# Half sums in four row groups, and rotation tables made behind the first head's key copies, in a two-layer diffusion backbone

## The chip, the core and the metric

The kernel runs on one NeuronCore of a Trainium2 chip. The metric is the device time of one execution in microseconds, as the median of several runs. TensorE (PE in the profile; its weight loads are PEld) multiplies, VectorE (DVE) and ScalarE (ACT) do the elementwise work, SyncE (SP) issues most of the DMAs, and ACT issues the others. GpSimd (POOL) only clears some buffers at the start. The program is written by hand, one instruction stream per engine, and the engines meet only at semaphores.

## The reference

```python
for i in range(DEPTH):                       # DEPTH = 2
    shift, scale, gate = adaln(c, ada_w[i], ada_b[i])
    shift_c, scale_c, gate_c = adaln(c_ctx, ada_w[i], ada_b[i])
    h = rmsnorm(x, norm_w[i]) * (1.0 + scale[:, None]) + shift[:, None]
    hc = rmsnorm(ctx, norm_w[i]) * (1.0 + scale_c) + shift_c
    if i % N_MIXERS == 0:
        y, yc = gla_mixer(h, hc, ...)        # layer 0: gated linear attention
    else:
        y, yc = diff_mixer(h, hc, ...)       # layer 1: differential softmax attention
    x = x + gate[:, None] * y
```

`adaln(cond, w, b)` is `silu(cond) @ w + b`, split into shift, scale and gate; `w` is 2048 x 6144 in each layer, and it is applied to two conditions, `c` and `c_ctx`. In layer 1 the queries and keys are normalised, multiplied by the weights `qn_w` and `kn_w`, and rotated: `t * cos + rot * sin`. There are 256 latent tokens and 256 context tokens, with 2048 features, all in float32.

## The kernel before

**Projections.** Each large product is cut into chunks of 512 output columns; a chunk has 8 pairs of 128 contraction rows. Chunks are numbered through the program: 0 to 11 are layer 0's projections (three for each of four heads), 12 to 15 its output product (`OUT0` = 12), 16 to 31 layer 1's projections (two for each of eight heads, `DIFF` = 16: keys and values, then queries and gates), and 32 to 35 its output product. In this text (16, 4) is pair 4 of chunk 16. Every weight pair goes through four steps: SP loads it into `w_raw`, ACT copies it, rounded, to `w_hi` (`split`, L558), DVE subtracts the two into `w_lo` (`low`, L1353), and PE multiplies (`project_pair`, L988). The buffers have four slots (`RING`), so that `split` of pair n+4 waits for PE to have finished pair n (`pair_done`), and PE's pair n waits for its `low` (`w_split`). A pair over four token tiles is 24 matmuls; one over two token tiles (queries and gates of layer 1) is 12. After a chunk the banks are copied out, and the next chunk's first matmul into a bank waits for `freed`.

**Modulation in the background.** Shift, scale and gate of layer 1, and the gate of layer 0, are made beside the projections. DVE multiplies tiles of `ada_w` (128 rows x 1024 columns, 512 KB) by the column of `silu(cond)` and adds them up in `ada_acc`, once for each condition m = 0, 1 (`weigh`, L1376 and L1378). One part of 2048 columns takes two halves of 1024 columns, each of 16 tiles; `HALVES` = 8 halves are numbered i = 0 to 7: gate of layer 0 (i = 0, 1), shift (2, 3), scale (4, 5) and gate (6, 7) of layer 1. SP loads tile m+2 only once DVE has weighed tile m (L411). When a half is complete, PE adds up its 128 partitions (`half_sums`, L948): four matmuls, for conditions m and column blocks b of 512, with a stationary operand of 32 columns of which one is all ones, and the results land in bank 7. In the kernel before the two conditions of a column block add into the same 32 rows of the bank, and even and odd halves use different row groups (0 and 32, or 64 and 96). Then either ACT copies the 64 rows to `ada_rows` (`half_rows`, L615, for i = 2 to 5) or DVE adds them to `gate_sums` (`add_half`, L1386, for the others). `column_sum` (L958) turns `ada_rows` into columns by a matmul with the selection matrix `sel`. `SUM_AT` says behind which pair PE does a half sum: (3, 3), (6, 1), (9, 1), (12, 1), (13, 5), (15, 3), (22, 6) and (28, 6). `SUM_OUT`, four pairs later in ACT's and DVE's order, is where the result is taken out. `COLUMNS_AT` puts the column sums behind (12, 5) and (15, 5).

**Into layer 1.** While PE does chunk 16 (keys and values of head 0), ACT and DVE make the modulated activations (`high1`, `remainder1`). Then ACT issues six small DMAs for cos, sin and the two normalising weights (L864 to L867), and waits for `rope_ok` before the first `split` of chunk 17. DVE waits for these DMAs (`rows_in`), multiplies the weights into the tables (L1743, and L1738 in `swapped`), signals `rope_ok`, and only then does `low` of (17, 0) to (17, 2) and copies out the banks of chunk 16 (`keys`, L1774). `silu_ag[:, 0]` holds the query weights until the tables are made, and is overwritten by the first Silu of head 0.

## Time and profile before

| | us |
|---|---|
| median of 3 runs | 1655.83 |
| range of the runs | 1652.74 to 1656.56 |
| the profiled execution | 1650.39 |
| its span, first to last instruction | 1648.6 |
| PE busy | 1591.9 |
| DVE busy | 1137.4 |
| ACT busy | 561.2 |

PE is busy nearly all the time, and its stretches of waiting are few and short. The columns of a timeline are start, duration, engine, line, operation, operands and count, with the idle time ahead of it in brackets; adjacent like instructions are merged. Matmul durations overlap, since they are pipelined: the time that one takes is the distance from its start to the next one's. A float32 matmul leaves two records, a matmul on float32r operands (L988) one.

### The profile page before, as it was taken

The page shows a single profiled execution, that of the slowest core. Times are in us where ns is not written, and L with a number is a line of the kernel's source. Part 1 is how long each engine was busy: PE and PEld are TensorE (multiplying, and loading weights), DVE is VectorE, ACT ScalarE, POOL GpSimd, SP SyncE. Part 2 cuts the span into 40 slices and gives each one's busy share as a digit, 9 for nine tenths or more (in the row PEclk, how much of TensorE's full clock was granted, in tenths as well). Part 3 has the DMA queues.
Part 4 walks back from the last instruction along what each step waited for, and adds up shares of the span by engine and source line. Part 5 has one row for each costly group of instructions (what it writes and reads, how often), then busy time and mean ns, then how long its engine had stood idle before and what let it go on. Part 6 is the DMA issues. An engine that isn't in the chain of part 4 may idle for free.

```text
span 1648.6 us, 18774 instructions
## 1 busy us (share of the span) xinstructions
PE 1591.9 (97%) x7392; PEld 1248.2 (76%) x7392; DVE 1137.4 (69%) x1720; ACT 561.2 (34%) x836; POOL 2.2 (0%) x9
## 2 busy tenths in 40 slices
PE   4899999999999999999999899999999999999998
PEld 2457877787778778867787677878777888788777
DVE  4338776877586659677796576777676768575864
ACT  4214332433243323532223333232323323232532
POOL 0000000000000000000000000000000000000000
PEclk9799999999999999999999899999999999999999
DMA  9993445345444354347765134445444454252554
GB/s 329 382 379 111 154 141 158 116 149 156 139 132 138 117 166 142 102 120 279 227 216 181 63 116 148 144 150 172 149 141 153 153 157 149 90 167 77 166 165 129
DMA packets 164228, 268.70 MB, mean 163 GB/s; under 512 B 11446, under 2 KB 95344, under 8 KB 162956
## 3 DMA queue, kind: packets, MB, share of 16 engines
q1 hardware_dynamic: 159072, 256.29, 48.3%
q10 hardware_dynamic: 5068, 11.22, 2.1%
q8 instruction: 58, 0.95, 0.2%
q14 instruction: 30, 0.25, 0.0%
HBM read 265.34 MB, written 2.12 MB: 162 GB/s over the span
## 4 chain that ended last, share of the span: by engine, by line
PE 86%; DVE 6%; DMA 5%; issue 1%; ACT 1%; SPq 1%; ACTq 1%; DVEq 0%
PE bank L988 68%; PE bank L1326 4%; DMA ada_w<-in_ada_w 3%; PE bank L1111 2%; PE bank L1164 2%; PE bank L1281 2%; PE bank L1265 2%; DVE ada_w L1378 1%; PE bank L924 1%; DVE w_lo L1353 1%; DMA u<-in_ctx 1%; PE bank L948 1%; DMA u<-in_ada_w 1%; PE bank L1107 1%; DVE work L1683 1%
## 5 line engine op out<-in xcount | busy, mean ns | idle before, releaser
L988 PE MATMUL bank<-w_lo,acts_hi 128*128 128x512 f32 x1536 | 613.8, 400 | 9.7 <-DVE work L1774 4.4
L988 PE MATMUL bank<-w_hi,acts_lo 128*128 128x512 f32 x1536 | 601.3, 391 | 0.0
L988 PE MATMUL bank<-w_hi,acts_hi 128*128 128x512 f32 x1536 | 601.1, 391 | 0.0
L558 ACT ACTIVATE w_hi<-w_raw 128x1024 fp32r<-128x1024 f32 x288 | 302.9, 1057 | 754.2 <-PE bank L988 673.8
L1353 DVE TENSOR_TENSOR w_lo<-w_raw,w_hi 128x1024 fp32r<-128x1024 f32 x288 | 350.3, 1221 | 277.5 <-ACT w_hi L558 277.1
L988 PEld LDWEIGHTS bank<-w_lo,acts_hi 128*128 128x128 f32 x1536 | 290.1, 189 | 85.9 <-issue 16.2
L988 PEld LDWEIGHTS bank<-w_hi,acts_lo 128*128 128x128 f32 x1536 | 290.1, 189 | 61.8
L988 PEld LDWEIGHTS bank<-w_hi,acts_hi 128*128 128x128 f32 x1536 | 290.5, 189 | 59.8 <-issue 1.9
L1378 DVE SCALAR_TENSOR_TENSOR ada_w<-ada_w,silu_p 128x1024 f32<-128x1024 f32 x210 | 261.4, 1280 | 27.2 <-DMA ada_w<-in_ada_w 23.9
L988 PE MATMUL bank<-acts_hi,w_lo 128*128 128x512 f32 x256 | 104.1, 407 | 4.3 <-DVE acts_lo L1472 4.3
L988 PE MATMUL bank<-acts_lo,w_hi 128*128 128x512 f32 x256 | 101.0, 395 | 0.0
L988 PE MATMUL bank<-acts_hi,w_hi 128*128 128x512 f32 x256 | 101.0, 395 | 0.0
L988 PEld LDWEIGHTS bank<-acts_hi,w_lo 128*128 128x128 f32 x256 | 49.0, 191 | 23.2 <-issue 13.5
L988 PEld LDWEIGHTS bank<-acts_hi,w_hi 128*128 128x128 f32 x256 | 49.1, 192 | 10.4 <-issue 0.7
L988 PEld LDWEIGHTS bank<-acts_lo,w_hi 128*128 128x128 f32 x256 | 48.8, 191 | 10.5
L1326 PE MATMUL bank<-w_lo,acts_hi 128*128 128x512 f32 x128 | 51.1, 399 | 4.3 <-DVE acts_lo L1804 3.6
L1326 PE MATMUL bank<-w_hi,acts_lo 128*128 128x512 f32 x128 | 49.9, 390 | 0.0
L1326 PE MATMUL bank<-w_hi,acts_hi 128*128 128x512 f32 x128 | 49.9, 390 | 0.0
L1164 PE MATMUL bank<-work 128*128 128x512 f32 x96 | 41.8, 592 | 0.0
L1111 PEld LDWEIGHTS bank<-work 128*64 128x64 f32 (+1 forms) x512 | 37.8, 150 | 4.9
L1111 PE MATMUL bank<-work 128*64 128x64 f32 (+2 forms) x512 | 40.7, 256 | 0.0
L1164 PEld LDWEIGHTS bank<-work 128*128 128x128 f32 x96 | 18.2, 190 | 21.4 <-issue 21.1
(185 smaller groups left out, 1247.4 us busy)
## 6 DMA issues: line engine op xcount, KB each, us to landing
ada_w<-in_ada_w SPq DMA_DIRECT2D x156, 512.0 KB, 4.4
w_raw<-in_diff_w_in SPq DMA_DIRECT2D x256, 256.0 KB, 3.0
w_raw<-in_gla_w_in SPq DMA_DIRECT2D x64, 512.0 KB, 3.8
w_raw<-in_gla_w_in SPq DMA_DIRECT2D x64, 256.0 KB, 3.1
u<-in_ada_w SPq DMA_DIRECT2D x32, 512.0 KB, 9.9
w_raw<-in_gla_w_out SPq DMA_DIRECT2D x32, 512.0 KB, 4.7
w_raw<-in_diff_w_out SPq DMA_DIRECT2D x32, 512.0 KB, 4.7
u<-in_x SPq DMA_DIRECT2D x2, 1024.0 KB, 6.5
```

Of the source, the lines that this page charges most:

```text
L558: act.activation(w_hi[:, p % RING], raw[:, p % RING], ACT.Copy).then_inc(w_hi_ok, 1)
L924: last = pe.matmul(bank[6 + q % 2][32 * j:32 * j + 32, :], silu_p[:, 2 * i + j // 2, :], quad_slot[slot][:, j, :], start=(i == 0), stop=(i ...
L948: last = pe.matmul(bank[7][row:row + 32, :], sel[:, 13 - m:45 - m], ada_acc[:, m, b * CW:(b + 1) * CW], start=(m == 0), stop=(m == 1 or i ...
L988: last = pe.matmul(bank[b][:], a, w, start=(k == 0 and i == 0), stop=(k == NK - 1 and i == 2))
L1107: pe.matmul(bank[4 + n % 3][:], a2[rows, (n % 2) * P:(n % 2 + 1) * P], zT[rows], start=True, stop=True).then_inc(logit_ok, 1)
L1111: return pe.matmul(out_, k_part, q_part, start=start, stop=True, skip_group_check=True)
L1164: last = pe.matmul(bank[4 + t][:], at[:, b, col:col + P], v_sb[:, kt, :], start=(i == 0), stop=(i == len(READ[t]) - 1))
L1265: pe.matmul(bank[4 + i][:], qT[:, m, t * P:(t + 1) * P], kT[:, m, :], start=True, stop=True)\
L1281: last = pe.matmul(bank[6][:, t * A_DV:(t + 1) * A_DV], aT[:, kt, t * P:(t + 1) * P], kv[:, kt, A_DV:CW], start=(kt == 0), stop=(kt == NT ...
L1326: last = pe.matmul(bank[b][:], a, w, start=(k == 0 and i == 0), stop=(k == NK - 1 and i == 2))
L1353: dve.tensor_tensor(w_lo[:, p % RING], raw[:, p % RING], w_hi[:, p % RING].bitcast(F32), ALU.subtract)\
L1378: last = dve.scalar_tensor_tensor(acc, ada_tile[:, m % 2], by, acc, ALU.mult, ALU.add)
```

## The change

Three things are changed.

1. `half_sums` gives each of the four (condition m, column block b) its own row group, 32 * (2m + b), and picks row i % 2 in it. Each matmul starts and ends its own sum. So the second half of a part lies in another row of the same groups, and the parts of a pair have to be added: the gate's rows are added by DVE over 128 partitions (64 for the last gate, which has one condition), and for shift and scale ACT copies the first half (i = 2, 4) and DVE adds the second (i = 3, 5) to `ada_rows`. `sel` and the rows of the biases follow (`sum_row`).
2. The rotation tables become a function, `rope_tables`, that DVE calls in `keys(0)`, behind the copies of the four banks and `low` of (17, 3).
3. ACT waits for `rope_ok` ahead of head 0's Silu, no longer ahead of the first `split` of chunk 17.

```diff
-BY_ACT = range(2 * SHIFT1, 2 * GATE1)
+BY_ACT = (2 * SHIFT1, 2 * SCALE1)
+
+def sum_row(j, cond):
+
+    return 32 * (2 * cond + j % 2) + j // 2
...
-                rows = slice(64 * (i % 2), 64 * (i % 2) + 64)
-                act.activation(ada_rows[rows], bank[7][rows], ACT.Copy).then_inc(half_out, 1)
+                act.activation(ada_rows[:], bank[7][:], ACT.Copy).then_inc(half_out, 1)
...
+                if h == 0:
+                    act.wait_ge(rope_ok, 1)
                 act.activation(silu_ag, qg[:, :, A_DV:CW], ACT.Silu).then_inc(g_ok, 1)
...
-            act.wait_ge(rope_ok, 1)
             attention_head(0, False)
...
                 for m in range(2 if i < 2 * GATE1 else 1):
                     for b in range(2):
-                        row = 32 * (2 * (i % 2) + b)
-                        last = pe.matmul(bank[7][row:row + 32, :], sel[:, 13 - m:45 - m],
-                                         ada_acc[:, m, b * CW:(b + 1) * CW], start=(m == 0),
-                                         stop=(m == 1 or i >= 2 * GATE1), skip_group_check=True)
+                        row = 32 * (2 * m + b)
+                        last = pe.matmul(bank[7][row:row + 32, :], sel[:, 13 - i % 2:45 - i % 2],
+                                         ada_acc[:, m, b * CW:(b + 1) * CW], start=True, stop=True,
+                                         skip_group_check=True)
...
             def add_half(i):
 
                 dve.wait_ge(half_sum, i + 1)
-                dve.wait_ge(gate_b_in, 8 * 16 * (1 if i < 2 else 2))
-                rows = slice(64 * (i % 2), 64 * (i % 2) + 64)
-                dve.tensor_tensor(gate_sums[rows], gate_sums[rows], bank[7][rows], ALU.add).then_inc(half_out, 1)
+                if 2 * SHIFT1 <= i < 2 * GATE1:
+                    dve.wait_ge(half_out, i)
+                    dve.tensor_tensor(ada_rows[:], ada_rows[:], bank[7][:], ALU.add).then_inc(half_out, 1)
+                else:
+                    dve.wait_ge(gate_b_in, 8 * 16 * (1 if i < 2 else 2))
+                    rows = slice(0, P if i < 2 else P // 2)
+                    dve.tensor_tensor(gate_sums[rows], gate_sums[rows], bank[7][rows], ALU.add).then_inc(half_out, 1)
...
-            dve.wait_ge(rows_in, 16 * 6)
-
...
-            for i, w in ((0, silu_ag[:, 0]), (2, knw)):
-                for t in range(2):
-                    dve.tensor_tensor(rope[:, i, t], rope[:, i, t], w, ALU.mult)
-                    last = swapped(rope[:, i + 1, t:t + 1], w.unsqueeze(1), rope[:, i + 1, t:t + 1])
-            last.then_inc(rope_ok, 1)
-            dve.wait_ge(rope_ok, 1)
+            def rope_tables():
+
+                dve.wait_ge(rows_in, 16 * 6)
+                for i, w in ((0, silu_ag[:, 0]), (2, knw)):
+                    for t in range(2):
+                        dve.tensor_tensor(rope[:, i, t], rope[:, i, t], w, ALU.mult)
+                        last = swapped(rope[:, i + 1, t:t + 1], w.unsqueeze(1), rope[:, i + 1, t:t + 1])
+                last.then_inc(rope_ok, 1)
+                dve.wait_ge(rope_ok, 1)
...
                 low(c + 1, 3)
+                if h == 0:
+                    rope_tables()
                 dve.wait_ge(freed[t], kv_freed(h, t) + 1)
```

DVE at the start of layer 1, before: the last `remainder1`, the tables (L1743, L1738), three `low`s of chunk 17, the copies of the banks, `low` of (17, 3) and the squares.

```order
L1717 SCALAR_TENSOR_TENSOR acts_lo<-work,mod,acts_hi 128x256
L1743 TENSOR_TENSOR work<-work 128x256 [waits rows_in]
L1738 TENSOR_TENSOR work<-work 128x4x32 x2
...
L1353 TENSOR_TENSOR w_lo<-w_raw,w_hi 128x1024 [waits w_hi_ok,rope_ok]
L1353 TENSOR_TENSOR w_lo<-w_raw,w_hi 128x1024 [waits w_hi_ok] x2
L1774 COPY work<-bank 128x512 [waits acc_ok] x3
L1774 COPY work<-bank 128x512 [waits pair_done]
L1353 TENSOR_TENSOR w_lo<-w_raw,w_hi 128x1024 [waits w_hi_ok]
L1762 TENSOR_TENSOR work<-work 128x1024 [waits freed3]
```

The same place after (the lines of the file have moved by some ten; L1753 and L1745 make the tables):

```order
L1726 SCALAR_TENSOR_TENSOR acts_lo<-work,mod,acts_hi 128x256
L1358 TENSOR_TENSOR w_lo<-w_raw,w_hi 128x1024 [waits w_hi_ok] x3
L1784 COPY work<-bank 128x512 [waits acc_ok] x3
L1784 COPY work<-bank 128x512 [waits pair_done]
L1358 TENSOR_TENSOR w_lo<-w_raw,w_hi 128x1024 [waits w_hi_ok]
L1753 TENSOR_TENSOR work<-work 128x256 [waits rows_in]
L1745 TENSOR_TENSOR work<-work 128x4x32 x2
...
L1772 TENSOR_TENSOR work<-work 128x1024 [waits freed3,rope_ok]
```

The tables have moved behind three `low`s, four copies and a fourth `low`; what stands behind them now is the squares of head 0's keys.

ACT at the same place, before: the last small DMA issues and the first `split`s of chunk 17.

```order
L865 DMA work<-in_diff_kn_w 128x256
L867 DMA work<-in_diff_qn_w 128x256
L558 ACTIVATE w_hi<-w_raw 128x1024 [waits pair_done,raw_in0,rope_ok]
L558 ACTIVATE w_hi<-w_raw 128x1024 [waits pair_done,raw_in1]
L558 ACTIVATE w_hi<-w_raw 128x1024 [waits pair_done,raw_in2]
L558 ACTIVATE w_hi<-w_raw 128x1024 [waits pair_done,raw_in3]
```

And after:

```order
L871 DMA work<-in_diff_kn_w 128x256
L873 DMA work<-in_diff_qn_w 128x256
L563 ACTIVATE w_hi<-w_raw 128x1024 [waits pair_done,raw_in0]
L563 ACTIVATE w_hi<-w_raw 128x1024 [waits pair_done,raw_in1]
L563 ACTIVATE w_hi<-w_raw 128x1024 [waits pair_done,raw_in2]
L563 ACTIVATE w_hi<-w_raw 128x1024 [waits pair_done,raw_in3]
```

The order is the same; only the wait for `rope_ok` has left the first of them.

DVE in chunk 12, layer 0's output product, before: `low` of (12, 4) and (12, 5), then the first tile of half 4 (L1376, both conditions) and the second (L1378).

```order
L1353 TENSOR_TENSOR w_lo<-w_raw,w_hi 128x1024 [waits w_hi_ok] x2
L1376 TENSOR_SCALAR ada_w<-ada_w,silu_p 128x1024 [waits weighed,tile_in0,half_sum]
L1376 TENSOR_SCALAR ada_w<-ada_w,silu_p 128x1024
L1378 SCALAR_TENSOR_TENSOR ada_w<-ada_w,silu_p 128x1024 [waits weighed,tile_in1]
L1378 SCALAR_TENSOR_TENSOR ada_w<-ada_w,silu_p 128x1024
```

And after:

```order
L1358 TENSOR_TENSOR w_lo<-w_raw,w_hi 128x1024 [waits w_hi_ok] x2
L1391 TENSOR_TENSOR ada_rows<-ada_rows,bank 128x512 [waits half_out,half_sum]
L1381 TENSOR_SCALAR ada_w<-ada_w,silu_p 128x1024 [waits weighed,tile_in0,half_sum]
L1381 TENSOR_SCALAR ada_w<-ada_w,silu_p 128x1024
L1383 SCALAR_TENSOR_TENSOR ada_w<-ada_w,silu_p 128x1024 [waits weighed,tile_in1]
L1383 SCALAR_TENSOR_TENSOR ada_w<-ada_w,silu_p 128x1024
```

The addition for half 3 has come ahead of the first tile of half 4; ACT's copy there (L615) is gone. The same addition for half 5 stands behind `low` of (15, 7).

## Rows read from the trace of the kernel before

**Rows 1.** The page's chain that ended last: share of the span by engine

```profile
PE 86%; DVE 6%; DMA 5%; issue 1%; ACT 1%; SPq 1%; ACTq 1%; DVEq 0%
```

**Rows 2.** The chain by pieces (start, us, what): first and last half sums

```profile
274.17 1.84 PE bank L948 x8
...
897.12 1.84 PE bank L948 x8
```

**Rows 3.** Timeline of PE at three startup products, four row groups each

```profile
86.08 1.92 PE L924 MATMUL bank<-ada_w,silu_p 128*32 128x512 f32 x16
87.82 1.04 PE L924 MATMUL bank<-u,silu_p 128*32 128x512 f32 x8
88.79 0.50 PE L988 MATMUL bank<-acts_hi,w_lo 128*128 128x512 f32 x1
```

**Rows 4.** Line L1386, DVE's gate additions: duration ns min/median/max, starts

```profile
L1386 DVE TENSOR_TENSOR gate_sums<-gate_sums,bank x4: 672/686/692, 276.5 to 1435.4; 64x512 f32<-64x512 f32 x4
```

**Rows 5.** The chain behind (12, 5)

```profile
743.36 1.42 DVE ada_w L1376 x2
...
744.79 12.76 DMA ada_w<-in_ada_w
```

**Rows 6.** Timeline of DVE: the low behind (15, 7)'s, with the idle time ahead of it

```profile
906.69 1.23 DVE L1353 TENSOR_TENSOR w_lo<-w_raw,w_hi 128x1024 fp32r<-128x1024 f32 x1 [8.46 <-ACT w_hi L558]
```

**Rows 7.** The page's DMA issues of weighing tiles: KB each, us to landing

```profile
ada_w<-in_ada_w SPq DMA_DIRECT2D x156, 512.0 KB, 4.4
```

**Rows 8.** Timeline of PE at the first bank that chunk 13 waits for

```profile
776.91 0.47 PE L988 MATMUL bank<-w_lo,acts_hi 128*128 128x512 f32 x1 [0.39 <-DVE work L1683]
```

**Rows 9.** Timeline of PE from chunk 16 to chunk 17

```profile
980.16 0.39 PE L988 MATMUL bank<-w_hi,acts_lo 128*128 128x512 f32 x1
984.35 0.77 PE L988 MATMUL bank<-w_lo,acts_hi 128*128 128x512 f32 x1 [3.80 <-DVE work L1774]
...
989.61 0.57 PE L988 MATMUL bank<-w_lo,acts_hi 128*128 128x512 f32 x1
990.01 0.40 PE L988 MATMUL bank<-w_hi,acts_hi 128*128 128x512 f32 x1
```

**Rows 10.** Busy time by stretch: seventh comes the granted clock, 1.00 is full

```profile
984.30:989.60 5.30, 5.25 (x12) 4.13 (x13) 5.23 (x7) 0.00 (x0) 0.00 (x0) 0.50 0.85 271
```

**Rows 11.** Waits from 960 to 1050 us: us in total, times, longest

```profile
DVE w_lo L1353 <- ACT w_hi L558: 15.9, 13, 4.1
ACT w_hi L558 <- DVE work L1738: 11.3, 1, 11.3
DVE work L1743 <- DMA work<-in_diff_qn_w: 7.3, 1, 7.3
```

**Rows 12.** The chain: the last small DMA, and DVE's start on the tables

```profile
971.11 4.73 DMA work<-in_diff_qn_w
...
975.86 0.42 DVE work L1743
```

**Rows 13.** Timeline of ACT: the first four splits of chunk 17

```profile
978.94 3.90 ACT L558 ACTIVATE w_hi<-w_raw 128x1024 fp32r<-128x1024 f32 x4 [11.28 <-DVE work L1738]
```

**Rows 14.** Timeline of DVE: lows of (17, 0) to (17, 6), bank copies

```profile
980.10 3.50 DVE L1353 TENSOR_TENSOR w_lo<-w_raw,w_hi 128x1024 fp32r<-128x1024 f32 x3 [1.20 <-ACT w_hi L558]
983.52 2.47 DVE L1774 COPY work<-bank 128x512 f32<-128x512 f32 x4
985.91 1.21 DVE L1353 TENSOR_TENSOR w_lo<-w_raw,w_hi 128x1024 fp32r<-128x1024 f32 x1
...
991.25 1.22 DVE L1353 TENSOR_TENSOR w_lo<-w_raw,w_hi 128x1024 fp32r<-128x1024 f32 x1 [0.24 <-ACT w_hi L558]
...
993.90 1.22 DVE L1353 TENSOR_TENSOR w_lo<-w_raw,w_hi 128x1024 fp32r<-128x1024 f32 x1 [0.21 <-ACT w_hi L558]
...
996.92 1.22 DVE L1353 TENSOR_TENSOR w_lo<-w_raw,w_hi 128x1024 fp32r<-128x1024 f32 x1
```

**Rows 15.** The chain: PE in head 1's queries and gates

```profile
1067.81 21.81 PE bank L988 x96
```

More of the change, by code:

```diff
@@ L417, in gate_biases @@
                     for cond in range(2):
-                        sp.dma_start(gate_sums[32 * j + cond:32 * j + cond + 1],
+                        sp.dma_start(gate_sums[sum_row(j, cond):sum_row(j, cond) + 1],
                                      io["ada_b"][layer:layer + 1, 2 * D + j * CW:2 * D + (j + 1) * CW])\
@@ L741, in gates_out @@
                     for j in range(4):
-                        row = 32 * j + cond
+                        row = sum_row(j, cond)
                         act.dma_start(gate_dram[layer, cond:cond + 1, j * CW:(j + 1) * CW], gate_sums[row:row + 1, :])\
@@ L1972, in constants @@
     part, row = np.arange(P) // 32, np.arange(P)[:, None] % 32
-    two, two_of_all = row == np.arange(4)[None, :] % 2, row == np.arange(8)[None, :] % 2
+    two = row == np.arange(4)[None, :] % 2
+    j_of, m_of = np.arange(8)[None, :] // 2, np.arange(8)[None, :] % 2
     return {
@@ L1979, in constants @@
         "sel": np.concatenate([two * (part[:, None] % 2 == np.arange(4)[None, :] // 2),
-                               two_of_all * (part[:, None] == np.arange(8)[None, :] // 2),
+                               (part[:, None] == 2 * m_of + j_of % 2) * (row == j_of // 2),
                                np.ones((P, 1)) * (np.arange(33)[None, :] == 1)], axis=1).astype(np.float32),
```

## The prediction

> **What bounds the kernel now.** I read the chain that ended last first, then PE's timeline where the chain leaves PE, then the waits around that place, then what stands behind the rows that the change moves. The chain is on PE for 86% of the span [rows 1]. So an edit pays if it takes time off PE in a stretch where nothing else is late, or if it removes a stop of PE. The change touches one of each.
>
> The half sums of half 0 at 274.17 us and of half 5 at 897.12 us are pieces of the chain, at 1.84 us each [rows 2]; so are those of halves 1, 2 and 4 between them, five such pieces in all. Half 3 is not: at its place the chain runs over DVE and a tile's DMA. Halves 6 and 7 have one condition and two matmuls, before and after, so nothing changes in them.
>
> The stop is where chunk 16 ends. The last matmul of (16, 7) starts at 980.16 us, and the first of chunk 17 at 984.35, released by a bank copy of DVE [rows 9]. Behind it PE's matmuls start 0.43 us apart instead of 0.227 until 990.01 [rows 9, 15]: the granted clock is 0.50 here, which is the lower of the two levels, 1.2 and 2.4 GHz [rows 10]. The reason for the stop is a queue. DVE waits 7.3 us for the last small DMA, makes the tables, and only then reaches three lows and the copies; ACT waits 11.3 us for the tables before its first split of chunk 17 [rows 11]. Neither needed the tables to do these things.
>
> **The half sums, on PE.** A startup product has the form that a half sum gets: four float32 matmuls of 32 columns by 512 into four different row groups. Two of them take 87.82 - 86.08 = 1.74 us, and the third, with PE's switch to the next kind of matmul, 88.79 - 87.82 = 0.97 us [rows 3]. A half sum before uses two groups twice and takes 1.84 us from start to start [rows 2]. So each saves 1.84 - 0.97 = 0.87 us, 0.97 being the one with the switch in it. Over five that is 4.35 us. The ends are 0 (the groups don't overlap in this form) and 0.97 a piece, or 4.85 us. I take 4.35, since the row has the same shapes, the same row groups and the same order.
>
> The Trainium skill has a rule that speaks against it. TensorE: Matmul & The Clock Gate, Part 3 (Packing small matmuls — row/col tiling), says that a weight load overlaps running matmuls only when its row group differs; here all four matmuls contract over the same 128 rows and differ only in their columns. By that rule nothing is gained, and the time would be 4.35 us above my forecast; the trace's startup products have the same form and run at 0.87 us each, which is against it.
>
> **The half sums, on ACT and DVE.** Two ACT copies, of halves 3 and 5, go; ACT is not late there, and I count nothing. The gate additions take the length of 512 elements over 128 partitions instead of 64; the trace has 0.69 us over 64 [rows 4], and the bank copies over 128 partitions take 2.47 us for four, 0.62 each [rows 14], so I count nothing there either. New are two additions on DVE, 0.69 us each by [rows 4]. The one of half 5 stands behind the low of (15, 7), where DVE then waits 8.46 us for ACT's next split [rows 6], and its cover is that wait; without it the addition would cost 0.69 us. The one of half 3 is ahead of the first tile of half 4, which is on the chain: two weighing instructions of 1.42 us, and then the load of the tile after next, which takes 12.76 us while the residual is loaded beside it [rows 5]. Queued behind the addition on DVE are these weighings and SP's load that waits for them, and later the bank copies for which PE stops 0.39 us at the head of chunk 13 [rows 8]. So it costs up to 0.69 us, or nothing if the load is held up by the bandwidth and lands when it would anyway. I take 0.3, the middle, and 0.87 us of PE's own gain at half 3 is lost in the same waits. If DVE weren't the late one there, that 0.87 would be gained as well; I keep it for the range.
>
> **The stop at 980 us.** ACT's last small DMA is issued by 971.6 us [rows 12], and the splits of (17, 0) to (17, 2) then wait only for PE to finish (16, 4) to (16, 6). A pair is 24 matmuls of 21.81 / 96 = 0.227 us, 5.45 us [rows 15]; counted back from 980.39, where (16, 7) ends, these pairs end at 964.0, 969.5 and 974.9. So the three splits are done by 976 and the three lows by 977.6, against 983.6 in the trace [rows 14]. DVE is then free when (16, 7) finishes its first tile, 9 matmuls before the end at 978.3, and the copies of banks 0 and 1, for which chunk 17 waits, are done by 979.8. The next matmul starts at 980.39 instead of 984.35: 3.96 us. The low clock goes with the stop: from 984.35 to 990.01 there are 13 matmuls in 5.66 us, which are 2.95 us at 0.227, so 2.71 us more [rows 9]. The sum is 6.67 us. The clock's part would be lost only with another stop in its place, which is a rival below.
>
> **What is late next.** The tables take from 975.86 to ACT's release at 978.94, 3.08 us [rows 12, 13]. Their DMAs have landed at 975.84 [rows 12], well ahead. They now stand between the low of (17, 3) and the squares of the keys, and behind these come the lows of (17, 4) to (17, 6), which PE needs. I lay them out from 980.39. ACT can split (17, 3) then, and DVE's low follows a split's start by 980.10 - 978.94 = 1.16 us [rows 13, 14], so it starts at 981.55. From one low to the next the trace has 5.34, 2.65 and 3.02 us [rows 14]; with 3.08 for the tables in the first distance, the lows of (17, 4), (17, 5) and (17, 6) start at 989.97, 992.62 and 995.64 and end 1.22 later: 991.19, 993.84, 996.86. A pair of chunk 17 is 12 matmuls, 2.73 us, so PE wants them at 991.30, 994.02 and 996.75. The margins are 0.1, 0.2 and -0.1 us. So PE may stop here for some tenths; I take 0.1 and keep 0.5 for the range. Behind that DVE's own waits for splits, 15.9 us between 960 and 1050 [rows 11], take up what is left of the delay, and head 0's key transposes come only behind the first pair of chunk 18.
>
> **The sum.** 4.35 + 6.67 - 0.1 - 0.3 = 10.6 us. The profiled execution took 1650.39 us, a span of 1648.6 and 1.8 around it, so that one would take 1639.8. Its time is 5.4 us below the median of the runs; the edits have nothing to do with that difference, so I take 10.6 off the median: 1645.2 us.
>
> **Rivals.** The tables turn the stop into another one. If the lows of (17, 4) to (17, 6) come over 1 us late, PE stops at each in turn for about 1.2 us in all, and if that costs the clock again, 2.71 us more: the gain is 10.6 - 1.1 - 2.71 = 6.8 and the time 1649.0. For it speaks that the margins are a tenth; against it, that stops of 0.39 us leave the matmuls at full pace [rows 8].
>
> The row groups don't overlap. Then the gain is 10.6 - 4.35 = 6.3 and the time 1649.6. Against it are the startup rows [rows 3].
>
> The stop stays. The change would not do what it says if the first splits of chunk 17 waited for something else, such as the raw weights or PE. Then the gain is 4.35 - 0.3 = 4.0, and the time 1651.8, within 0.3%. For it: a wait is put down to what came last, and so the trace doesn't show what stood behind the tables. Against it: the four splits take 3.90 us without a gap once the tables are done, so all else that they wait for had come by then [rows 13].
>
> The slower side: the added DVE work in chunk 12 moves the weighing of half 4's first tile, and so the tile loads, further into the residual's load. A tile's load there takes 12.76 us [rows 5] and 4.4 in the median [rows 7], so each further tile caught costs up to 8.4 us. One would leave 2.2 us of the gain; from the second on the kernel is slower, at 1645.2 + 16.8 = 1662.0. Against it: a shift of 0.69 us is small beside the 12.76, and the residual's load doesn't start later.
>
> **How the numbers follow.** About 0.3%, 5.0 us, is what a measurement of this kernel can tell from no change. My forecast has 0.72, the second stop 0.09, no overlap 0.06, the stop that stays 0.09, two tiles caught 0.02, and 0.02 is for what I don't see. The first three are faster by over 0.3%: 0.87. Within it: 0.10. Slower: 0.03. The forecast's own bounds are 6.67 + 4.85 + 0.87 = 12.4 us of gain at the most, and 4.35 + 6.67 - 0.5 - 0.69 = 9.8 with all costs: 1643.4 to 1646.0, and some 1.5 us of scatter of a median, since the three runs lie within 3.8. Upwards the range takes in the second stop and the missing overlap: 1642.0 to 1650.0.
>
> **What the profile after would show.** The half sums of halves 0 to 5 each take 0.97 us to PE's next start. The stop ahead of chunk 17 is gone or below 0.3 us, and the granted clock is 1.00 from 975 to 1000 us. ACT's splits of (17, 0) and (17, 1) stand right behind the small DMAs. The tables stand behind four bank copies and a low, and PE's waits in chunk 17 are some tenths on the lows of (17, 4) to (17, 6). The tile load behind (12, 5) is issued 0.7 us later against PE's pair. The prediction is wrong if PE's stop of 0.1 us becomes several, if the half sums keep 1.84 us, or if the chain in chunk 12 grows by more than 1 us.

## The result, and the profile after

| | us |
|---|---|
| after, median of 4 runs | 1640.26 (1639.18 to 1641.13) |
| before, median of 4 runs beside them | 1654.28 (1649.32 to 1656.56) |
| ratio after / before | 0.9922, interval 0.9908 to 0.9937 |
| the profiled execution after, and its span | 1640.21, 1638.4 |
| span before | 1648.6 |

The kernel became 0.8% faster. The sign and the mechanism were as forecast, but the time lies 1.7 us below the lower end of the range (1642.0). Between the two profiled executions the span differs by 10.2 us; the sum said 10.6. One execution in the runs below, of run 10, took 2397.82 us at a mean granted clock of 0.625, and it stands in no comparison.

The page after, PE's busy time and the chain by engine. The columns are as in [rows 1]:

```profile
PE 1584.0 (97%) x7392; PEld 1244.2 (76%) x7392; DVE 1138.1 (69%) x1722; ACT 560.1 (34%) x834; POOL 2.2 (0%) x9
...
PE 84%; DMA 6%; DVE 6%; issue 1%; ACT 1%; SPq 1%; ACTq 0%; DVEq 0%
```

DVE and ACT have as much work as before; PE is busy 7.9 us less.

**The half sums.** Timeline of PE after at the sum of half 0, which answers to [rows 2]:

```profile
270.68 1.07 PE L953 MATMUL bank<-ada_w,sel_sb 128*32 128x512 f32 x8
271.68 0.50 PE L993 MATMUL bank<-acts_hi,w_lo 128*128 128x512 f32 x1
```

The next matmul starts 1.00 us behind the sum's start, where it was 1.84. The four matmuls now overlap. The weight loads (PEld) show the same. After, all eight (a float32 matmul leaves two) stand together at the start of the sum, beside its running matmuls:

```profile
270.68 0.16 PEld L953 LDWEIGHTS bank<-ada_w,sel_sb 128*32 128x32 f32 x8 [0.35 <-issue]
```

Before, four stood there and the other four came in two pairs later, 0.43 us apart:

```profile
274.09 0.14 PEld L948 LDWEIGHTS bank<-ada_w,sel_sb 128*32 128x32 f32 x4 [0.35 <-issue]
274.55 0.12 PEld L948 LDWEIGHTS bank<-ada_w,sel_sb 128*32 128x32 f32 x2 [0.31 <-issue]
274.98 0.12 PEld L948 LDWEIGHTS bank<-ada_w,sel_sb 128*32 128x32 f32 x2 [0.31 <-issue]
```

**The way into chunk 17.** Timeline of DVE after, which answers to [rows 14]; L1784 copies the banks, L1358 is `low`, L1753 and L1745 make the tables, L1772 begins the squares:

```profile
973.99 2.73 DVE L1784 COPY work<-bank 128x512 f32<-128x512 f32 x4 [1.02 <-PE bank L993]
977.18 1.23 DVE L1358 TENSOR_TENSOR w_lo<-w_raw,w_hi 128x1024 fp32r<-128x1024 f32 x1 [0.46 <-ACT w_hi L563]
978.33 0.41 DVE L1753 TENSOR_TENSOR work<-work 128x256 f32<-128x256 f32 x1
...
980.88 0.48 DVE L1745 TENSOR_TENSOR work<-work 128x128 f32<-128x128 f32 x2
981.40 1.23 DVE L1772 TENSOR_TENSOR work<-work 128x1024 f32<-128x1024 f32 x1
...
985.62 1.23 DVE L1358 TENSOR_TENSOR w_lo<-w_raw,w_hi 128x1024 fp32r<-128x1024 f32 x1 [0.24 <-ACT w_hi L563]
...
987.96 1.22 DVE L1358 TENSOR_TENSOR w_lo<-w_raw,w_hi 128x1024 fp32r<-128x1024 f32 x1
```

Timeline of ACT after, which answers to [rows 13]: the last small DMA issue and the four splits.

```profile
966.55 0.45 ACTq L873 DMA_DIRECT2D work<-in_diff_qn_w  x1
967.11 2.01 ACT L563 ACTIVATE w_hi<-w_raw 128x1024 fp32r<-128x1024 f32 x2 [4.01 <-issue]
970.65 1.06 ACT L563 ACTIVATE w_hi<-w_raw 128x1024 fp32r<-128x1024 f32 x1 [1.53 <-PE bank L993]
976.09 1.06 ACT L563 ACTIVATE w_hi<-w_raw 128x1024 fp32r<-128x1024 f32 x1 [4.38 <-PE bank L993]
```

Two splits stand right behind the DMA issues, and the others wait only for PE's pairs. The chain of waits after, over the same stretch, which answers to [rows 9]:

```profile
937.88 48.99 PE bank L993 x216
986.87 0.03 issue
986.90 16.62 PE bank L993 x72
```

PE runs through 288 matmuls; the only seam is at pair (17, 4), whose `low` begins at 985.62. The chain gives it 0.03 us of waiting, but the starts show more:

```profile
986.48 0.39 PE L993 MATMUL bank<-w_hi,acts_lo 128*128 128x512 f32 x1
986.90 0.50 PE L993 MATMUL bank<-w_lo,acts_hi 128*128 128x512 f32 x1
987.23 0.40 PE L993 MATMUL bank<-w_hi,acts_hi 128*128 128x512 f32 x1
```

Two distances of 0.42 and 0.33 us stand where matmuls are otherwise 0.227 apart, so the seam costs 0.30 us. Busy time from 960 to 1000 us after; the seventh figure, 1.00, is the granted clock (0.91 in the same stretch before), which answers to [rows 10]:

```profile
960.00:1000.00 40.00, 39.97 (x177) 32.78 (x176) 31.95 (x55) 15.10 (x19) 0.00 (x0) 1.00 0.52 162
```

**Chunks 12 and 13.** The chain after behind (12, 5), which answers to [rows 5]; L1391 is the new addition of half 3:

```profile
738.81 0.68 DVE ada_rows L1391
739.49 1.34 DVE ada_w L1381 x2
740.83 0.02 issue
740.84 12.40 DMA ada_w<-in_ada_w
```

Timeline of PE after at the head of chunk 13, which answers to [rows 8]:

```profile
772.78 0.47 PE L993 MATMUL bank<-w_lo,acts_hi 128*128 128x512 f32 x1 [1.55 <-DVE work L1692]
...
774.02 0.50 PE L993 MATMUL bank<-w_lo,acts_hi 128*128 128x512 f32 x1 [0.30 <-DVE work L1692]
```

Here the stop grew from 0.39 to 1.55 us, and the clock fell behind it:

```profile
772.00:776.00 4.00, 2.78 (x8) 1.53 (x9) 3.90 (x8) 1.83 (x5) 0.00 (x0) 0.82 0.76 262
776.00:780.00 4.00, 4.00 (x15) 3.03 (x14) 3.96 (x6) 1.45 (x4) 0.00 (x0) 0.75 0.40 81
```

**Where the 10.2 us lie.** PE's timeline has places that every kernel here passes: the first gate logits matmul of layer 0's heads 0 to 3 (L0 to L3), the starts of the half sums (h0 to h7), and the row sum of layer 1's input (rs; L1240 before, at 929.16 us). The distance from each to the next is worked out from their start times. The first column of numbers is the kernel before; the others are what the same distance is longer (+) or shorter (-) by. e2 and e12 are the changed kernel run again, e3 has the sums alone, e4 the tables alone (all below).

```
from -> to   before    after      e2     e12      e3      e4
 0 -> L0     138.13    -0.25   +2.89   +0.22   +2.25   +0.62
L0 -> h0     135.97    -3.17   -1.61   -3.15   -0.03   +0.04
h0 -> L1      25.70    -0.87   -0.87   -0.88   -0.87   +0.01
L1 -> h1     121.98    +0.01   -0.01    0.00   -0.01   +0.01
h1 -> L2      36.59    -0.88   -0.88   -0.89   -0.88   -0.01
L2 -> h2     121.98    +0.01   +1.60   +1.61   -0.01    0.00
h2 -> L3      36.58    -0.87   -0.88   -0.87   -0.87    0.00
L3 -> h3     121.98    +1.61    0.00   -0.01   +1.61   +0.01
h3 -> h4      74.56    +0.88   +0.92   -0.33   +0.33   +0.22
h4 -> h5      83.58    -0.88   -0.88   -0.86   -0.87    0.00
h5 -> rs      32.11    -0.86   -0.85   -0.86   -0.86   -0.01
rs -> h6     277.40    -4.85   -5.77   -7.17   -1.02   -6.24
h6 -> h7     227.75    +0.12   -0.34   -0.63   +0.45   -0.25
h7 -> end    208.42    -0.19   -0.14   -0.20   -0.14   -0.03
```

Five rows, those that begin with h0, h1, h2, h4 and h5, hold nothing but a half sum that gains 0.87 us: 4.36 in all. The row h3 -> h4 holds half 3's sum and what was lost for it. The row rs -> h6 holds the stop at 980 us, the weighing of half 6, and the start of chunk 16, which nobody changed and which differs between executions: from rs to pair 1 of chunk 16 PE takes 13.05 us before, and +0.70, +0.64, -0.59, -0.97 and -0.05 us against that in the five other columns. Without it the row is -5.55, -6.41, -6.58, -0.05 and -6.19. The rows L0 -> h0 to L3 -> h3 hold what nobody changed: the gate logits and the projections behind them. There the differences come in steps of 1.6 us. They are a low clock that some executions have and others don't. Timeline of PE before at head 0's logits:

```profile
138.13 4.03 PE L1107 MATMUL bank<-gate_zT,gate_a 32*128 32x512 f32 x8 [0.78 <-DVE gate_zT L1584]
142.10 0.80 PE L988 MATMUL bank<-w_lo,acts_hi 128*128 128x512 f32 x1
142.69 0.63 PE L988 MATMUL bank<-w_hi,acts_hi 128*128 128x512 f32 x1
143.12 0.63 PE L988 MATMUL bank<-w_hi,acts_lo 128*128 128x512 f32 x1
```

And after:

```profile
137.88 3.08 PE L1112 MATMUL bank<-gate_zT,gate_a 32*128 32x512 f32 x8 [0.78 <-DVE gate_zT L1593]
140.90 0.50 PE L993 MATMUL bank<-w_lo,acts_hi 128*128 128x512 f32 x1
141.23 0.40 PE L993 MATMUL bank<-w_hi,acts_hi 128*128 128x512 f32 x1
```

The same work, matmuls 0.43 us apart in the one and 0.23 in the other. The clock fell while the logits were still running: they take 3.97 us to the next start before, and 3.02 after. At head 3 it is the changed kernel that has the low clock (+1.61):

```profile
612.00:616.00 4.00, 3.94 (x11) 1.97 (x9) 3.79 (x7) 3.11 (x6) 0.00 (x0) 0.77 0.02 4
616.00:620.00 4.00, 4.00 (x15) 3.17 (x15) 3.97 (x10) 3.84 (x8) 0.00 (x0) 0.80 0.01 2
```

### The profile page after: what moved, and what is told of

The parts are those of the page before. It is cut to its first block, busy times and chain, and to the rows that moved or that the text cites. A ratio compares the mean times of both kernels' runs of the same rounds, so it can differ in the third digit from the quotient of the medians.

```text
span 1638.4 us, 18776 instructions
## 1 busy us (share of the span) xinstructions
PE 1584.0 (97%) x7392; PEld 1244.2 (76%) x7392; DVE 1138.1 (69%) x1722; ACT 560.1 (34%) x834; POOL 2.2 (0%) x9
## 4 chain that ended last, share of the span: by engine, by line
PE 84%; DMA 6%; DVE 6%; issue 1%; ACT 1%; SPq 1%; ACTq 0%; DVEq 0%
PE bank L993 68%; DMA ada_w<-in_ada_w 5%; PE bank L1331 4%; PE bank L1116 2%; PE bank L1169 2%; DVE ada_w L1383 2%; PE bank L1286 2%; PE bank L1270 2%; PE bank L929 1%; DMA u<-in_ctx 1%; DMA u<-in_ada_w 1%; DVE w_lo L1358 1%; PE bank L1112 1%; DVE work L1692 1%; DVE u L1694 1%
## 5 line engine op out<-in xcount | busy, mean ns | idle before, releaser
L1358 DVE TENSOR_TENSOR w_lo<-w_raw,w_hi 128x1024 fp32r<-128x1024 f32 x288 | 350.0, 1221 | 272.0 <-ACT w_hi L563 271.4
L575 ACT ACTIVATE stat<-stat 128x4 f32<-128x4 f32 (+2 forms) x30 | 6.2, 206 | 83.6 <-DVE stat L1420 83.5
```

The source lines that it names most:

```text
L1358: dve.tensor_tensor(w_lo[:, p % RING], raw[:, p % RING], w_hi[:, p % RING].bitcast(F32), ALU.subtract)\
```

## The experiments

The theory is the prediction's: 0.87 us for each sum, 6.6 for the stop and its clock, little lost in chunk 12. The rivals are that the profiled execution before was a lucky one, that one of the two edits brings nearly all, that the tables' cover is not where I laid it, and that chunk 12's tile load eats part of the sums. From the ninth run on it is also asked what the low clocks at the logits are worth. Four kernels shared one chip and its runs of the kernel before in each of the first two groups, three in the third, two in the last.

**1 and 2. Both kernels again.** No edit.

> The kernel before, unchanged, timed against itself. The profiles of before and after differ by 10.2 us of span (1648.6 and 1638.4), the medians of their runs by 14.0. Theory A (scatter): the edits give about 10, and the kernel before has short stretches at the low clock in places that differ from run to run (its profile has one at 140 to 147 us, the one of after has two, at 612 to 620 and 772 to 780). Then this kernel's runs scatter by some 4 to 8 us, its profile shows such stretches at other places, each costing 1.5 to 3.5 us, and its median is 1650 to 1655. Theory B (the profile of before was the odd one): its runs stay within 2 us of 1654 and the profile's span is near 1653, with the 4 us at fixed places.

> The changed kernel, unchanged. Theory A: its median is 10 to 12 us below that of the kernel before on this chip, about 1640 to 1642, and its profile has the low-clock stretches at other places than 612 and 772 us. Theory B: the distance is 13 to 14 us again, and these two stretches are at the same places.

The kernel before took 1652.1 us (1646.85 to 1657.25, 12 runs), against 1653.0 in the runs beside it (0.9996, interval 0.9984 to 1.0009). The kernel after took 1642.61 (1640.19 to 1645.9, 6 runs), 0.9929 (0.9912 to 0.9947). So one kernel spreads over more than 10 us, and the 1655.83 that I subtracted from was high. The new trace of the kernel before has a span of 1649.1 us, and its low clocks stand at the same places as in the first one (at head 0's logits, at rs and at the stop), so the first profiled execution was no odd one; that the places would differ, as my theory A had it, did not come. In the new trace of the kernel after they stand at the logits of heads 0 and 2 and at the head of chunk 13, where the first one had them at head 3 and at chunk 13. Over all runs that stood beside the experiments, the kernel before has a mean of 1653.2 us (79 runs, a standard deviation of 2.3); the kernel after has 1641.1 (15 runs, 2.3). The difference is 12.1, and by these spreads it is uncertain by 1.3 us (twice 2.3 times the root of 1/79 + 1/15).

**3. The sums alone.** The kernel before with the diff's part 1.

> The four row groups alone; the tables stay where they were. By the two traces each of five half sums gains 0.84 us: 4.2 us, less some tenths for the added DVE work in chunk 12. Theory A: 3.5 to 4.5 us faster, with the stop of 3.8 us at the end of chunk 16 and the low clock behind it unchanged. Theory B (an effect beside the terms): 7 or 8 us.

1646.71 us (1643.99 to 1649.54, 6 runs), 0.9958 (0.9942 to 0.9974). The stop at the end of chunk 16 is unchanged:

```profile
983.21 0.77 PE L992 MATMUL bank<-w_lo,acts_hi 128*128 128x512 f32 x1 [3.81 <-DVE work L1782]
```

The ratio is 6.9 us, with an interval from 4.3 to 9.6; the steps' sum for this part, 4.05, lies just outside. By the table the five sums give 4.35, and h3 -> h4 loses 0.33, which is 4.0; the trace's other differences belong to no sum (+2.25 in the startup, +1.61 of a low clock at head 3, -0.97 at the start of chunk 16). Why the median gained more than the steps isn't shown. The stop at the head of chunk 13 is 1.61 us here as well, but the clock didn't fall behind it.

**4. The tables alone.** The kernel before with parts 2 and 3.

> The tables behind the first head's key copies and ACT's wait moved, the half sums as before. By the two traces the gain from the end of chunk 16 to head 1 is 6.4 us, and some 0.9 are given back by half 6's weighing in heads 1 and 2. Theory A: 5.0 to 6.5 us faster, no stop at the end of chunk 16 and no low clock there. Theory B: 9 or more.

1648.07 us (1644.2 to 1651.12, 8 runs), 0.9961 (0.9947 to 0.9975). The half sums keep their old time, 1.85 us from start to start:

```profile
274.76 1.91 PE L949 MATMUL bank<-ada_w,sel_sb 128*32 128x512 f32 x8
276.61 0.50 PE L989 MATMUL bank<-acts_hi,w_lo 128*128 128x512 f32 x1
```

From pair 1 of chunk 16 to pair 1 of chunk 18 PE takes 72.89 us before, 72.79 in run 1 and 72.87 in run 3. It is 66.52 here, 66.50 after and 66.55 in run 2. The tables' edit is worth 6.35 us, with or without the other one. By the ratios each edit alone brings some 6.5 us and both together 11.7; no interplay can be seen within these intervals.

**5. The tables twice.** `rope_tables` issues its instructions a second time, onto buffers that are free there; the output is unchanged.

```diff
                 dve.wait_ge(rows_in, 16 * 6)
+                for n, w in ((0, silu_ag[:, 0]), (2, knw)):
+                    for t in range(2):
+                        dve.tensor_tensor(k_t[:, n + t], rope[:, 0, t], w, ALU.mult)
+                        swapped(k_n[:, n + t:n + t + 1], w.unsqueeze(1), rope[:, 1, t:t + 1])
```

> The changed kernel with the tables' 12 instructions issued a second time ahead of the real ones, onto scratch rows: 3.05 us more on DVE between the low of (17, 3) and the keys' squares; the output doesn't change. If the cover of the tables ends where the prediction's layout says (PE wants the low of (17, 4) within 0.1 us of when it comes), PE stops 2.9 to 3.1 us ahead of (17, 4), and if a stop of that length costs the clock, matmuls behind it start 0.43 us apart for some 5 us: 3 to 5.7 us more than the changed kernel, half or more of what the move of the tables gained. If there was slack that the layout overlooked, the stop is under 2 us.

1647.75 us (1644.59 to 1649.05, 5 runs), 0.9959 (0.9945 to 0.9973). PE now stops at (17, 4), and the clock falls:

```profile
991.03 0.50 PE L993 MATMUL bank<-w_lo,acts_hi 128*128 128x512 f32 x1 [2.98 <-DVE w_lo L1358]
...
992.30 0.44 PE L993 MATMUL bank<-w_hi,acts_lo 128*128 128x512 f32 x1
992.54 0.63 PE L993 MATMUL bank<-w_lo,acts_hi 128*128 128x512 f32 x1
...
995.94 0.40 PE L993 MATMUL bank<-w_hi,acts_lo 128*128 128x512 f32 x1
```

The stretch takes 71.11 us, 4.6 more. Three more microseconds of DVE gave 2.98 of stop: the cover behind the copies is used up by one set of tables, as the margins of 0.1 to 0.2 us said, and a second set costs its whole length and the clock.

**6. Only ACT's wait moved.** The kernel before, with part 3 of the change alone: the tables stay in front.

```diff
+                if h == 0:
+                    act.wait_ge(rope_ok, 1)
                 act.activation(silu_ag, qg[:, :, A_DV:CW], ACT.Silu).then_inc(g_ok, 1)
...
-            act.wait_ge(rope_ok, 1)
             attention_head(0, False)
```

> The kernel before with only ACT's wait for the tables moved behind its splits; DVE makes the tables where it did. ACT's splits of chunk 17 then stand ahead of the tables, so the low of (17, 0) starts when the tables end, not 1.16 us later. If DVE's queue (DMA wait 7.3, tables 3.1) is the cause of the stop, the stop shrinks from 3.8 to 2.6 us, the low clock behind it stays: 1.1 to 1.3 us faster in the trace from head 0 to head 0, too little for the median. If ACT's wait was the cause, the stop is gone: 6 us faster.

1653.42 us (1648.78 to 1657.26, 10 runs), 0.9991 (0.9978 to 1.0003): no difference.

```profile
988.73 0.77 PE L989 MATMUL bank<-w_lo,acts_hi 128*128 128x512 f32 x1 [2.99 <-DVE work L1775]
...
991.42 0.45 PE L989 MATMUL bank<-w_lo,acts_hi 128*128 128x512 f32 x1
991.71 0.39 PE L989 MATMUL bank<-w_hi,acts_hi 128*128 128x512 f32 x1
```

The stop is 2.99 instead of 3.80, and the stretch 70.78, 2.1 less. The low clock behind the shorter stop was shorter too. The larger part of the gain, 4.3 of 6.35 us, comes from DVE's copies no longer waiting for the DMAs and the tables. The median shows nothing of the 2.1; this execution had the low clock behind the logits of all four heads, and its mean granted clock was 0.981.

**7. Tables in two parts.** The keys' tables stay where the change put them, the queries' go behind two `low`s of chunk 18. `rope_tables` gets the row and the weight as arguments, and ACT's wait ahead of the Silu is for both parts.

```diff
-                    rope_tables()
+                    rope_tables(2, knw)
...
+                if h == 0:
+                    rope_tables(0, silu_ag[:, 0])
                 low(c + 1, 2)
```

> The changed kernel with the queries' tables (6 of the 12 instructions) moved on into the queries' part of head 0. The trace after shows only 0.03 us of waiting ahead of (17, 4), so by the layout nothing is left to gain: within 0.1 us in the trace from chunk 16 to chunk 18, the median within the scatter of the changed kernel. If the stretch had hidden waits, up to 0.5 us.

1642.76 us (1640.04 to 1643.59, 4 runs), 0.9929 (0.9914 to 0.9945). The stretch takes 66.20 us, 0.3 less than after; in the median that can't be seen. The two matmuls at (17, 4) are 0.23 us apart here, so these 0.3 us are the seam, and they are what the tables still cost PE in their new place. My 0.1 was too small, and it came from the wait that the chain shows.

**8. A tile's weighing later.** One weighing of half 4 is moved from the end of chunk 12 into chunk 13, away from the bank copies for which PE stops.

```diff
 WEIGH_AT = weigh_table()
+WEIGH_AT[70] = (OUT0 + 1) * PAIRS + 3
```

> The changed kernel with one weighing tile (tile 6 of half 4) taken from behind the low of (13, 1) to behind that of (13, 3), 2.48 us less on DVE ahead of the copies of chunk 12's banks. Theory C: the four row groups turned 0.84 us of PE's gain at half 3 into a longer stop at the first bank of chunk 13 (0.39 to 0.66 us without them, 1.55 to 1.66 with them), long enough that the clock drops behind it in two of three profiles. Then the stops there shrink from 2.2 or 2.6 us to about 0.8, the clock stays at 1.00 around 776 us, and the time is 1.5 to 3.5 us below the changed kernel's. Rival: DVE isn't what holds the banks, and it is the same.

1641.85 us (1639.92 to 1643.24, 6 runs), 0.9926 (0.9914 to 0.9939). The stops at the head of chunk 13 fell to 0.25 and 0.37 us with the clock at full, but PE then waited for the half to be complete:

```profile
814.89 1.06 PE L954 MATMUL bank<-ada_w,sel_sb 128*32 128x512 f32 x8 [2.60 <-DVE ada_w L1384]
```

From h3 to h5 it is 0.41 us shorter than before, where the changed kernel is at 0.00, 0.04 and -1.19 in its three traces. In this trace half 4 has no slack: what PE doesn't wait for at one end it waits for at the other. The 1.5 to 3.5 us expected did not come.

**9. Half 4's sum a pair later.** Run 7's and run 8's edits, and the sum moved with the weighing.

```diff
+WEIGH_AT[70] = (OUT0 + 1) * PAIRS + 3
+WEIGH_AT[80] = (OUT0 + 2) * PAIRS + 3
 SUM_AT = [WEIGH_AT[NK * i + NK - 1] - 2 for i in range(HALVES)]
+SUM_AT[4] += 1
```

> The tables split as in e7, the tile moved as in e8, and half 4's sum on PE one pair later, behind (13, 6), with half 5's first tile behind the low of (14, 3). In e8 the stops at chunk 13's banks shrank to 0.6 us, but PE then waited 2.60 us for the weighing ahead of half 4's sum. If that wait is all that ate the gain, PE has neither wait now: from half 3's sum to the transposes behind (13, 3) about 58.5 us as in e8, and from there to behind half 4's sum no wait above 0.3 us; 2 to 3.5 us below the changed kernel. If DVE is simply full from 743 to 815 us, the wait turns up at another place and the time is within 1 us of the changed kernel's.

1640.28 us (1638.73 to 1643.58, 6 runs), 0.993 (0.9912 to 0.9948). From h3 to h5: 3.30 - 4.16 = -0.86. The wait ahead of the sum is gone, but PE stops 1.09, 0.30, 0.35 and 0.36 us for banks at the head of chunk 15, where it stopped once for 0.37 before; from start to start PE takes 2.2 us more there. By its time it isn't told apart from the kernel after. This trace reached the first logits only at 142.85 us, 4.72 later than before, in a part that no kernel here changes.

**10. The logits apart.** The gate logits of a head in two halves, with pair 0 of the next projection between them, to see whether the low clock behind them goes. `gate_logits` gets the matmuls that it is to do as an argument.

```diff
-                gate_logits(h)
+                gate_logits(h, (0, 2))
                 project(c + 1, lambda t: c + 1, True,
-                        after=lambda p: unit_scores(h, 0) if p == 5 else None)
+                        after=lambda p: unit_scores(h, 0) if p == 5 else gate_logits(h, (1, 3)) if p == 0 else None)
```

> The changed kernel with the gate logits of each layer-0 head issued as two and two, the second two behind pair 0 of the values' chunk, instead of four in a row. Theory D: the scatter of all these kernels comes from short low-clock stretches behind places where PE does little: behind the four logits (32 rows of contraction, 3.1 us) the clock was low in 9 of 10 traces at head 0, and in 1, 4 and 3 of 10 at heads 1, 2 and 3, at 1.7 to 3 us each. With 1.5 us at a time the stretches at 140, 300, 460 and 620 us are gone or rarer, the median is 2 to 5 us below the changed kernel's and the runs lie closer together. If the stretches come by chance wherever PE is, they stay at these places or come at others, and the time is the same.

1647.89 us (12 runs, 11 of them from 1646.33 to 1652.81), 0.9977 (0.9964 to 0.999). So it is slower than the kernel after. The low clock is gone from all four places, as here at head 0:

```profile
137.00:145.00 8.00, 7.45 (x32) 5.03 (x32) 1.25 (x2) 1.90 (x3) 0.00 (x0) 1.00 0.01 2
```

but PE has a new wait, for ACT's work on the later logits:

```profile
PE bank L993 <- ACT work L703: 8.5, 4, 2.7
```

The four stops are 1.83, 2.26, 1.71 and 2.68 us long, and behind the second and the fourth, at 348 and 669 us, the clock is low instead. So L1 -> h1, L2 -> h2 and L3 -> h3 are 3.9, 1.7 and 4.1 us longer than before: the stop alone in the second, the stop and 1.6 us of low clock in the others. That the four logits matmuls in a row bring the clock down is borne out in so far as it fell at none of these places in the two traces where they are apart (this and run 11's); but four traces with the four in a row (after's and those of runs 9, 12 and 13) had none at head 0 either, so two traces are a weak support. That taking it away pays is refuted for this order.

**11. All three edits.** Runs 9 and 10 together.

> e9 and e10 together. If both hold: 4 to 8 us below the changed kernel, 1633 to 1638.

1647.12 us (1644.04 to 1650.77, 10 runs), 0.9963 (0.995 to 0.9976). The 1633 to 1638 us expected did not come: the waits for ACT are 10.2 us in four stops, and behind two of them (2.97 and 2.53 us) the clock is low.

**12 and 13. The kernel after and run 9's once more, on one chip.**

> The changed kernel once more. So far it was 14.0 us below the median of the kernel before in the first comparison and 10.4 in the second; the two profiles differ by 10.2 us of span. Theory A (the edits give 10 to 10.5, and the rest is which runs had how many low-clock stretches): about 10 to 12 us below the kernel before here, and at equal mean granted clock 9 to 10.5 us below it. Theory B (a further effect of the change that neither the half sums nor the tables show in the traces): 12.5 to 15, and more than 11.5 at equal clock.

> The kernel of e9 once more, beside the changed kernel on the same chip. By the traces it gains 0.9 us over it from half 3's sum to half 5's, 0.3 us from chunk 16 to chunk 18, and it spares the low clock at the head of chunk 13 where that comes: 1 to 3 us below the changed kernel. If the gain of e9 was scatter, the two are within 0.7 us.

The kernel after: 1641.55 us (1636.36 to 1642.29, 5 runs), 0.9928 (0.9914 to 0.9942). By its ratio the kernel after is 11.9 us below the kernel before, which lies in theory A's range and not in theory B's. Run 9's kernel: 1637.71 (1636.42 to 1642.14, 5 runs), 0.9915 (0.99 to 0.993). The intervals overlap, and both profiled spans are 1634.6 us. Run 9's kernel beats the kernel before by 0.85% here. Whether it beats the changed one stays open: 3.8 us between the medians of five runs here, but 1.2 between their means, and 1.2 between the means of all runs of the two; 0.86 us less than before from h3 to h5 in the first trace and 1.66 in the second, against 0.00, -0.04 and 1.19 after.

The windows of run 12's kernel show an execution with the clock at full where the first one after lost it, at the head of chunk 13, though PE stopped there for 0.95 us:

```profile
772.00:776.00 4.00, 2.71 (x9) 1.46 (x9) 3.90 (x7) 2.38 (x6) 0.00 (x0) 1.00 0.72 251
776.00:780.00 4.00, 3.64 (x16) 2.92 (x16) 3.96 (x5) 1.33 (x4) 0.00 (x0) 1.00 0.29 91
```

## Why the prediction was right, and where it was wrong

**The half sums: right.** 0.87 us each was the forecast from [rows 3]; the table shows 0.87 at each of the five that pay, 4.36 against 4.35. The row groups overlap although all four matmuls contract over the same 128 rows. Four groups of 32 output columns suffice: 1.00 us against 1.84. Where TensorE: Matmul & The Clock Gate, Part 3, of the Trainium skill lets loads overlap only with a different row group, the trace decides against it here: the eight loads of a sum take 0.16 us in all, beside its matmuls over the same 128 rows. That rule speaks of loads, and "by that rule nothing is gained" was my own step. The same Part 3 of the Trainium skill lists three tiles of 32 columns beside each other as 2.38 times as fast, a case that no run here has, so it did not speak against the change as a whole.

**The stop: right.** 6.67 us was the forecast; 6.35 is measured, and 66.50 to 66.56 us for the stretch in four traces (after, runs 2, 4 and 8). Of the missing 0.3 us, run 7 gives 0.3 back when half of the tables go elsewhere. So it is what the tables cost behind `low` of (17, 3), and 0.1 was taken for it. The layout held within 0.3 us. `low` of (17, 3) was laid out at 981.55 and came at 977.18, and with the same shift of 4.37 the next two are expected at 985.60 and 988.25; they came at 985.62 and 987.96. Run 5 shows that nothing more would have fitted. "The stop stays" fell with it.

**Half 3's addition: not contradicted, but not resolved either.** 0.3 us was taken, and half 3's own 0.87 given up. The addition takes 0.68 us. The tile load behind it took 12.40 us instead of 12.76, and landed 0.1 us later against half 3's sum. But over the fifteen traces this load is issued 5.9 to 7.6 us behind the start of the sum and lands 18.1 to 19.3 us behind it, and in the four traces without the addition it lands at 18.5 to 19.0. So it landed about when it would anyway, as the lower bound said, and the addition's own cost is lost in what executions differ by. The row h3 -> h4 is +0.88, +0.92, +0.33 and -0.33 in four traces that have the edit, and +0.27, +0.22 and +1.46 in runs 1, 4 and 6, which don't. The stop at the head of chunk 13 is 0.95 to 2.31 us in the seven traces with the edit and the old order of weighing (after, runs 2, 3, 5, 7, 10 and 12), and 0.39, 0.66, 0.60 and 1.28 in the four without it. So it is longer with the edit, but run 6 shows that it grows in some executions without it too. A low clock came with it in after and in runs 2, 5 and 6. After beside run 3, with stops of 1.55 and 1.61, puts that at 0.55 us; but run 7's trace has +0.92 without a low clock, so this price isn't clean. My sentence that short stops leave the clock alone rested on one stop of 0.39 us [rows 8], and holds only for such. No tile more was caught by the residual's load (two loads over 10 us before and after), and the slower side did not come.

**How the numbers follow: wrong.** The miss is 1645.2 - 1640.26 = 4.9 us, and the step that failed is "I take 10.6 off the median". The miss has three parts. The three runs' median, 1655.83, lay 2.5 us above the median of 79 later runs, 1653.3. The gain between the pooled means is 12.1 us and not 10.6, which is 1.5, little more than its uncertainty of 1.3. And the four runs after lay 0.9 below the median of 15, 1641.1. I had allowed 1.5 us of scatter "since the three runs lie within 3.8". One execution spreads by 2.3 us (standard deviation), over 11 us from end to end. The trace that I had read held the warning: the profiled execution was 5.4 us below the median, and I wrote that off as nothing to do with the edits.

**What the 1.5 us are** is only partly settled. The runs' mean granted clock is 0.9828 before and 0.9851 after. That is 1.7% and 1.5% of the time lost, 28.4 and 24.5 us, worked out as share times time. Of these 3.9 us the low clock around the old stop, from 983.1 to 990.0 us in the trace of before, is 3.4 (half of 6.9), and the part of it that slowed PE, 2.7, is counted in the sum. The other 0.5 may be the places that come and go: in the three traces after, the low clock behind head 0's logits was missing in two and cost half as much in one, and in the two of the kernel before it was there in full. But each of the three had one at a later head (+1.6), which those two had not. Whether the edits, by shifting times, change how often it falls there, or whether these are draws, fifteen runs and three traces don't tell. What the rest of the 1.5 us is, if it isn't scatter, no run shows. At equal clock the difference is 9.8 us (0.982 to 0.984: 50 runs before, 4 after) and 10.2 (0.985 to 0.988: 12 and 11). That was close to 10.6; but at equal clock the stop's 2.7 us should not count in full, so this comparison can't be taken as a confirmation of the sum either.

**The rivals.** A second stop, no overlap, the stop that stays and two tiles caught are excluded by the rows above. None of my cases ended below 1643.4, because each was a mechanism of the edits; none was the measurement's own.

## What to carry to other kernels

A run of four small products over the same rows was cheaper here in four column groups of the array than in two (1.00 us against 1.84), with the parts added elsewhere; and work that only one later step needs belongs behind the copies that free the banks, after its length has been laid against the next instruction that PE waits for. A forecast of under 1% should put the width of the baseline's own scatter on both ends of its range: here the profiled execution lay 5.4 us below the median of three runs, and the median turned out 2.5 us too high. Comparing places that both traces pass told in one table what no median could: which 0.87 us were the edit and which 1.6 us were not.

## What the runs showed of the hardware that was not expected

- The clock can fall at work without a stop. At the four logits matmuls of a head, which contract over 32 rows, and behind them it was low for about 1.6 or 3.2 us worth of PE time in some executions and full in others of one kernel. Head 0 had it in the trace of before and those of runs 1 to 8, but not in after's nor in those of runs 9, 12 and 13. Of the same traces two had it at head 1 (runs 6 and 9), six at head 2 and three at head 3. Ahead of head 0's logits PE waits 0.78 us in all of them, ahead of the other heads' not at all. Whether the logits are the cause isn't shown beyond run 10.
- The same stop is followed by a low clock in one execution and not in another. At the head of chunk 13 it fell behind stops of 1.28, 1.55, 1.66 and 2.31 us and not behind 0.95, 1.60, 1.61 and 1.75. At the stops for ACT in runs 10 and 11 it fell behind 2.26, 2.53, 2.68 and 2.97 and not behind 1.71, 1.83, 2.21 and 2.51, and not behind run 8's 2.60. A stop of 1.97 us near the end (at 1592 us before) stands in all fifteen traces, and the clock fell behind it in two, those of runs 5 and 9. The five stops of 3 to 3.8 us at chunks 16 and 17 were all followed by it.
- The startup, up to the first logits, took 137.6 to 142.9 us in fifteen traces, with the same instructions. This, the clock's places of 1.6 us and the start of chunk 16 are what the traces of one kernel mostly differ by.
- A 512 KB load beside the residual's load landed at about the same time in all fifteen traces, whether it was issued early or late: it was issued 5.9 to 7.6 us behind the start of half 3's sum, took 12.8 to 11.0 us, and landed 18.1 to 19.3 us behind that start.
